# Reordering the latent attention's start, the gate's inner layer by tokens, and a store by half rows

## The reference

```
# RWKV: the output gate
xg = x + (x_prev - x) * mu[5]
g = sigmoid(xg @ g1) @ g2            # g1: 1024 x 160, g2: 160 x 1024
...
out = ((yn + bonus) * g) @ w_o
# MLA: latents and queries
down = rmsnorm(x, kv_norm_g) @ kv_w_down      # 256 latents + 32 rotary
c_kv = rmsnorm(down[..., :256], kv_a_norm_g)
up   = c_kv @ kv_w_up                          # keys and values of 16 heads
c_q  = rmsnorm(h @ q_w_down, q_norm_g)         # 384 latents
q    = c_q @ q_w_up
...
return x + rmsnorm(ffn(x), g)                  # stored as (256, 1024) f32
```

## Time and profile before

| what | value |
|---|---|
| median of 3 runs | 1152.27 us (lowest 1151.79) |
| the profiled execution | 1150.95 us, of which 1149.1 us are its span |
| PE busy | 1128.2 us, 98% |
| DVE, ACT, POOL busy | 69%, 48%, 14% |
| mean granted clock of TensorE | 0.998 |

### The profile page before, as it was taken

How to read it: one execution, slowest core, us unless ns; L and a number is a source line. 1 busy time by engine, 2 the same in 40 slices (tenths; PEclk the granted TensorE clock), 3 DMA queues, 4 the chain that set the end, 5 groups by cost and what they waited for, 6 DMA issues and landing times.

```text
span 1149.1 us, 19373 instructions
## 1 busy us (share of the span) xinstructions
PE 1128.2 (98%) x7698; PEld 1029.0 (90%) x7698; DVE 790.6 (69%) x1088; ACT 548.1 (48%) x776; POOL 166.2 (14%) x211
## 2 busy tenths in 40 slices
PE   7999999999999999999999999999999999999997
PEld 6997899899998788989999988998779879999986
DVE  7989898777775648857777646687678776344443
ACT  6765344444443556845344344644544445333332
POOL 0141101111111011001111100550000001111100
PEclk9999999999999999999999999999999999999999
DMA  8553251646666656426666564554350446666551
GB/s 236 166 167 104 88 169 39 155 121 184 183 183 226 208 131 134 142 77 177 183 183 181 190 260 151 182 185 136 120 142 25 151 165 158 183 184 178 197 194 74
DMA packets 218099, 181.34 MB, mean 158 GB/s; under 512 B 42673, under 2 KB 196766, under 8 KB 218030
## 3 DMA queue, kind: packets, MB, share of 16 engines
q1 hardware_dynamic: 215422, 171.63, 50.0%
q0 software_dynamic: 2032, 6.88, 1.8%
q10 hardware_dynamic: 576, 1.87, 0.5%
HBM read 177.73 MB, written 2.62 MB: 157 GB/s over the span
## 4 chain that ended last, share of the span: by engine, by line
PE 87%; DVE 7%; ACT 3%; issue 2%; DMA 1%; POOL 1%; DVEq 0%; POOLq 0%; ACTq 0%; SPq 0%
PE bank L272 23%; PE bank L274 23%; PE bank L273 23%; PE bank L1298 2%; DVE ring L386 1%; PE bank L344 1%; PE bank L1165 1%; PE bank L2577 1%; PE bank L358 1%; PE bank L2590 1%; PE bank L2522 1%; ACT arena L380 1%; PE bank L2544 1%; PE bank L1267 1%; PE bank L1279 1%
## 5 line engine op out<-in xcount | busy, mean ns | idle before, releaser
L272 PE MATMUL bank<-arena,arena 128*128 128x256 f32 (+2 forms) x1868 | 593.4, 318 | 3.2 <-DVE ring L386 1.2
L386 DVE TENSOR_TENSOR ring<-ring,arena 128x2048 fp32r<-128x2048 f32 (+1 forms) x136 | 305.2, 2248 | 157.1 <-ACT arena L380 156.1
L380 ACT ACTIVATE arena<-ring 128x2048 fp32r<-128x2048 f32 (+1 forms) x143 | 269.0, 1884 | 289.9 <-DMA ring<-in_ffn_w_in 109.3
L272 PEld LDWEIGHTS bank<-arena,arena 128*128 128x128 f32 x1868 | 356.0, 191 | 29.0 <-issue 3.7
L273 PE MATMUL bank<-arena,arena 128*128 128x256 f32 (+1 forms) x1308 | 373.3, 285 | 0.0
L274 PE MATMUL bank<-arena,ring 128*128 128x256 f32 x1220 | 345.2, 283 | 0.0
L273 PEld LDWEIGHTS bank<-arena,arena 128*128 128x128 f32 x1308 | 250.8, 192 | 1.1
L274 PE MATMUL bank<-arena,arena 128*128 128x512 f32 (+3 forms) x644 | 239.3, 372 | 0.0
L274 PEld LDWEIGHTS bank<-arena,ring 128*128 128x128 f32 x1220 | 234.1, 192 | 0.0
L273 PE MATMUL bank<-ring,arena 128*128 128x512 f32 (+2 forms) x560 | 216.1, 386 | 0.0
L274 PEld LDWEIGHTS bank<-arena,arena 128*128 128x128 f32 x644 | 121.2, 188 | 20.8
(11 more groups left out here) (343 smaller groups left out, 1371.4 us busy)
## 6 DMA issues: line engine op xcount, KB each, us to landing
ring<-in_ffn_w_in SPq DMA_DIRECT2D x80, 512.0 KB, 5.0
ring<-in_ffn_w_out SPq DMA_DIRECT2D x44, 512.0 KB, 4.5
ring<-in_w_gate_up SPq DMA_DIRECT2D x40, 512.0 KB, 5.0
ring<-in_w_in SPq DMA_DIRECT2D x18, 1024.0 KB, 5.0
ring<-in_a_w_rkv SPq DMA_DIRECT2D x12, 1024.0 KB, 5.2
ring<-in_w_down SPq DMA_DIRECT2D x22, 512.0 KB, 3.8
ring<-in_a_w_o SPq DMA_DIRECT2D x4, 1024.0 KB, 9.5
arena<-in_ffn_w_in SPq DMA_DIRECT2D x8, 512.0 KB, 4.6
```

Source lines behind the costliest of these rows:

```text
L272: nc.tensor.matmul(dst, stationary[0], moving[0], start=start, stop=False)
L380: nc.scalar.activation(buf(hi_of(n), 0, w, arena12), ring[:, r, 0:w], ACT.Copy).then_inc(hi_ready, 1)
L386: on.tensor_tensor(ring12[:, r, 0:w], ring[:, r, 0:w], buf(hi_of(n), 0, w, arena12).bitcast(F32), ALU.subtract).then_inc(split_ready, 1)
```

## The change

On PE, the gate's inner layer moves ahead of the first round of `pairs`, and its operands are swapped: 128 tokens are stationary and the 160 columns of g1 move, so its result has tokens in rows. ACT takes the sigmoids into `gated`, with the last 32 columns of each tile written twice; three transposes after eight banks of `pairs` turn it, and ACT copies it to `lora` after nine. Two `keep_busy` matmuls go. DVE makes the keys and the bonus product before its masks instead of after them, and masks the first round's copies (`added_masked(0)`) after the second round's masks. ACT copies the first two banks of values out one step before the values are complete. In MLA, `xn_turns` moves from before the last query projection of tile 0 into its middle, one weight subtraction is cut in halves around the latents, and three steps of DVE and ACT are put in another order. The store is made in four halves, the last from ACT's queue.

More of the change, by code:

```diff
@@ L1204, in rwkv_pe @@
             w = weights(pe, FIRST["lora_g2"])
-            pe.wait_ge(r_evac, 4)
-            pe.wait_ge(cols_ready, 2)
-            keep_busy(pe, 2, 2)
-            pe.wait_ge(gate_hidden, 1)
-            for q in (1, 2, 3, 0):
+            pe.wait_ge(gate_hidden, 3)
+            for q in (0, 2, 3, 1):
                 a, half = q // 2, q % 2
-                if q == 0:
-                    pe.wait_ge(gate_hidden, 2)
+                if q == 1:
+                    pe.wait_ge(cols_ready, 2)
                 nc.tensor.matmul(bank[q][:, :], lora[:, 2 * T + a * P:2 * T + (a + 1) * P],
@@ L1453, in rwkv_act @@
             ahead(act, FIRST["w_v"] + 1, split_act)
[L1454 to L1459, removed]
             for j in range(4):
@@ L1627, in rwkv_dve @@
                                         spread(const("before").unsqueeze(1), [P, 2, P]), ALU.mult).then_inc(n_masked, 1)
[L1628 to L1631, removed]
             ahead(dve, FIRST["w_v"] + 1, split_dve)
@@ L2242, in kv_weights_lo, with kv_half_lo @@
             def kv_weights_lo(s):
+                kv_half_lo(s, 0, SLOT).then_inc(xs_split, 1)
+            def kv_half_lo(s, lo, hi):
                 dve.wait_ge(xs_hi, KV_SPLIT0 + s + 1)
-                nc.vector.tensor_tensor(buf(KV_W[s], mem=arena12), buf(KV_W[s]), buf(KV_W_HI[s], mem=arena12).bitcast(F32),
-                                        ALU.subtract).then_inc(xs_split, 1)
+                return nc.vector.tensor_tensor(buf(KV_W[s], lo, hi, arena12), buf(KV_W[s], lo, hi),
+                                               buf(KV_W_HI[s], lo, hi, arena12).bitcast(F32), ALU.subtract)
             variance(0, 0, 2)
```

## The result

The changed kernel takes **1144.13 us** (median of 5 runs, 1143.31 to 1144.58) against 1151.79 for the kernel before beside it; the ratio is 0.9934, 95% interval 0.9923 to 0.9945. Forecast were 1145.3, range 1142.3 to 1149.5. The profiled execution of the changed kernel took 1144.13 with a span of 1142.2; of before 1150.95 and 1149.1. The difference of the spans, 6.8 (1149.08 - 1142.24 before the pages round them), is what has to be explained. One of the five executions of the kernel before took 3950.46 us; in a median of five it weighs no more than any other long one.

The account below looks back on a forecast made before the run. PE, busy 98% of the span, was taken as the bound. RWKV 3.54 + MLA 3.1 + store 0.4 = 7.0 us off 1150.95 gives 1143.9; the median's 1.3 above that makes 1145.3, range 1142.3 to 1149.5.

Parts of the forecast that it names:

- The rival in which the weight load sets the pace: Gate's inner layer: loading 128 stationary columns sets the pace, so 2.6 us are lost, giving 1147.9; chance 0.08.
- The two waits: RWKV's `pairs` rounds: PE's stops of 0.22 and 0.40 us, one per round, both go, saving 0.62.
- The solve: DVE's solve before the second `pairs` round: begins at 99.0, ends at 126.7, 0.2 us after PE wants the first mask.
- PE is four banks ahead: cost nothing: Second `pairs` round: the first mask comes 0.2 us late, but PE's lead over it makes that free.
- The rival of a late solve: Second `pairs` round: from 126.7 on each us of lateness costs one; 2 us late gives 1147.3; chance 0.15.
- the five places: First 30 us of MLA: PE's waits of 0.74, 0.67, 0.38, 0.54 and 0.86 us; 3.1 us forecast saved.
- Step (3): MLA, PE's 0.38 us wait before the key projection: DVE starts earlier, half of it, 0.19, goes.
- step (5): MLA, PE's wait before the second `q_nope`: one DVE subtraction moves behind what PE needs, so 0.86 us goes.
- (4): MLA, PE's wait for the odd heads' keys: their copies now precede three lo parts, so 0.54 us goes.
- the rival that leaves (4) and half of the rest: MLA: waits mostly move on; only the odd heads' keys wait and half the others go, 1147 to 1147.5; chance 0.12.
- The store: Kernel's end: the last DMA carries 256 KB and lands 2.2 us after issue, saving 0.4, at best 0.7.
- TensorE's clock: Between the gate's inner layer and the values: rival that the clock falls; 20 us of it give +16, 1161; chance 0.03.

Follow-up runs that it names:

- copy_late: Changed kernel with ACT's copy of the turned gate behind twelve banks of the first `pairs` round instead of nine; 1145.53 us, ratio 0.9954.
- mask_first: Changed kernel with DVE's product over the first masked matrices back between the solve and the second round's masks; 1147.02 us, ratio 0.996.
- split_and_store: Changed kernel with the last `q_up` subtraction again before the queries' first odd heads, and all four result halves stored from SP; 1145.42 us, ratio 0.9942.
- products_late: Changed kernel with DVE's two products (keys, bonus) behind the first round's masks again; 1145.74 us, ratio 0.9945.
- gate_by_columns: Changed kernel with the gate's inner layer in its new place but old form: 256 moving columns, no transposes, no copy; 1147.03 us, ratio 0.9959.
- columns_again: Changed kernel with the gate's inner layer in its new place but old form (256 moving columns), without fillers, profiled a second time; 1146.14 us, ratio 0.9955.

## Why the prediction was right, and where it was off

The mechanism held: 6.8 in the stretches against 7.0, with PE the bound and nothing given back downstream. The parts were off in both directions, so that the sum came nearer than its terms: RWKV gave 0.7 less, MLA and the store together 0.5 more.

- *The gate's inner layer*: 7.17 - 4.44 = 2.73 saved, 2.61 forecast, 0.139 a record against 0.140. The rival in which the weight load sets the pace is dead: by columns in the same place the records take 0.222.
- *Transposes and fillers*: +0.48 and -0.55, against +0.33 and -0.64. Three transposes between other matmuls cost more than 3/16 of a row of 16.
- *The two waits*, 0.62 forecast. The step failed at its first half. The wait of 0.22 went, but the round became 0.28 longer (8.95 against 8.67 between starts). In its first half, where the wait had stood, only 0.04 was gained (4.31 against 4.35); in the second 0.32 was lost (4.64 against 4.32). "ACT's sigmoids cost nothing unless ACT falls four banks behind" left out the copy of the turned gate (L1468, 0.49), which the change puts between ACT's copies of the banks; `copy_late` showed that it costs 0.32, and its round of 8.63 is still only 0.04 under the kernel before's. The round is a loop PE to DVE to ACT to PE, with little slack, and not a queue four banks deep. Of the 0.40, 0.24 went. RWKV gave 2.8, not 3.54.
- *The solve*: start 99.14 (99.0), end near 126.9 (126.7). "PE is four banks ahead: cost nothing" had the price nearly right, 0.16, and the reason wrong: the four banks are used up by then, and `mask_first` charged 2.30 for 2.28. The rival of a late solve had its rate right, one for one.
- *MLA*: 3.4 against 3.1. At the five places PE gained 0.49, 0.83, 0.48, 0.78 and 0.83, where 0.65, 0.67, 0.19, 0.54 and 0.86 were listed. Step (3) was mis-sized at 0.19, half of its wait; all of it went. `split_and_store` shows that the move of step (5) is worth 1.44 in the changed kernel: once (4) is gone, its wait would have grown. Three of my sums don't come out. The first is 0.04 in the forecast, the others enter neither it nor its range: 0.74 - 0.05 is 0.69 and not 0.65; (4), (5) and half of the rest make 2.2, where I took 1.9 as the low end; and the rival that leaves (4) and half of the rest, 1.7 of 3.1, gives 1146.7 and not 1147 to 1147.5.
- *The store*: 0.56 against 0.4. Interpolated between 64 KB and 512 KB the size had given 2.2; it landed at 2.0 to 2.1. The estimate of 0.6 by the Trainium skill, DMA: Bandwidth & Descriptors, Anatomy of one DMA, was the better one here. That holds for its slope alone: the page's fit is for DMAs that GpSimd issues, and its 2.0 us plus bytes gives 3.2 for 512 KB and 2.6 for 256 KB, where 2.6 and 2.0 to 2.1 were measured.
- *The median*: the 1.2 between forecast and result come from the 1.3 that I added for the median over the profiled execution. That median had 3 runs, one of them the 3950.46; later ones of before, over 5 to 23 runs, are 1151.2 to 1151.8, and the changed kernel's profiled execution is its own median. Against 1143.9, the forecast for an execution like the profiled one, the result is 0.2 off.
- *TensorE's clock*: given 0.03, with a price of 16 us. Neither profile of the changed kernel showed it before PE's end. But it fell in five of the other twelve profiles, each time for 3.4 us, and in A and B at a price of 1.4 to 1.6. Two falls came 1.1 us after PE had taken up work from a long pause: in the second round after 2.46 (mask_first), and in the start after 2.08 (split_and_store, lower from 15.6 to 19.1), where the other thirteen profiles show a pause of 1.5 to 1.6 and no fall. Three came at the first values, where no pause over 0.24 stood in front, so "no wait of PE reaches 1 us" was no protection. Nor is the fall a matter of the new place alone. The mean granted clock of each execution tells more: 0.997 stands beside four of the five profiles with a fall (0.998 beside the fifth) and beside none without one. The kernel before has 0.997 in 8 of the 45 executions measured beside the experiments, all of them among the 15 that took 1152.7 or more; the other 30 took 1149.8 to 1151.7. So it seems to fall there too, though its one profile shows no fall. By columns in the new place, with fillers or without, it is 7 of 14 executions, of the changed kernel none of 10. That speaks for a chance that depends on what stands in front of the values; no profile shows what decides.

## What to carry to other kernels

Where an engine's copies close a loop back to PE, an instruction put among them costs PE time, however idle that engine is (0.32 for a copy of 0.49): put it behind the last copy that PE still waits for. When a side chain (here the solve) ends within 0.2 us of PE, stop shortening PE's part: price the chain, whose lateness now costs one for one (2.46 for 2.49 in products_late, 2.30 for 2.28 in mask_first). And read differences of parts of a per cent from stretches between fixed rows of a trace, since start and DMA waits alone scatter by more.

## What the runs showed of the hardware

- POOL's float32 product of 128x2048 takes 4.53 us, and 6.50 where 2.1 us of it (80.83 to 82.95) lie beside DVE's product of two SBUF operands: it took 1.97 longer, so it nearly stood still beside it, while DVE's 2.29 is what the same product takes elsewhere (2.28). The Trainium skill, GPSIMD Engine Reference, Specifications, says that the two share SBUF interfaces and contend when DVE has two SBUF inputs; the trace agrees, and puts the whole price on POOL, whose product began 0.17 after DVE's. No trace here shows the other order.
- TensorE's granted clock fell to 0.50 (1.2 GHz) for 3.4 us with no pause of PE over 0.05 in the 20 us in front of it, and of two profiles of one program (gate_by_columns, columns_again) in one only. A comparison by single runs carries that 1.6 us.
